# Reordering the weighing of v in a PEER layer: coefficient work, gathers and the loads of v

## The reference, cut to what matters

```
u = peer_u[ix]
a = gelu(einsum('td,thkd->thk', hx, u))
vsel = peer_v[ix]
out = einsum('thk,thkd->td', gx * a, vsel)
```

## Time and profile before

| | |
|---|---|
| median of 3 runs | 3344.83 us (3337.7 to 3346.16) |
| profiled execution | 3339.36 us, its span 3337.5 us |
| TensorE matmuls busy | 2777.6 us, 83% of the span |
| weight loads busy | 1940.9 us, 58% |
| DVE, ScalarE, Pool busy | 1414.0, 847.5, 982.1 us |
| weighing of v, first to last matmul | 1231 to 1777 us |

### The profile page before, as it was taken

The page is one execution under the profiler, slowest core; times in us unless marked ns, Lnnn a source line. Parts: engine busy times, 40 slices in busy tenths (PEclk is TensorE's granted clock), DMA queues, the critical chain, the costliest instruction groups (busy, mean ns, idle before and its releaser), DMA issues. The chain is left out here.

```text
span 3337.5 us, 34889 instructions
## 1 busy us (share of the span) xinstructions
PE 2777.6 (83%) x12909; PEld 1940.9 (58%) x12909; DVE 1414.0 (42%) x2354; ACT 847.5 (25%) x1423; POOL 982.1 (29%) x480
## 2 busy tenths in 40 slices
PE   5985697999999969999995967985788887887886
PEld 3853587998999957777774845664322232222222
DVE  3346527995777755667655254433000000100001
ACT  1224212334666623333333203221100000000001
POOL 0030003667777758887781020000000000000000
PEclk7977798999999989999997975566999999999999
DMA  5343113546999989999993120012899999999996
GB/s 218 103 154 112 69 62 113 170 164 230 335 333 356 350 313 342 341 341 332 334 344 128 57 70 13 1 54 108 349 421 421 422 421 421 421 421 421 421 421 281
DMA packets 267733, 866.91 MB, mean 260 GB/s; under 512 B 30911, under 2 KB 118591, under 8 KB 214968
## 3 DMA queue, kind: packets, MB, share of 16 engines
q1 hardware_dynamic: 211008, 700.59, 55.5%
q0 software_dynamic: 38016, 138.43, 11.0%
q10 hardware_dynamic: 18584, 26.23, 2.1%
HBM read 809.56 MB, written 55.61 MB: 259 GB/s over the span
## 5 line engine op out<-in xcount | busy, mean ns | idle before, releaser
L675 PE MATMUL dots_dot_ps<-one_acts,dots_u_split 128*128 128x384 f32 x3072 | 554.8, 338 | 21.8 <-POOL dots_u_split L87 21.4
L802 PE MATMUL val_banks<-val_v,val_coef_split 128*128 128x512 f32 x2304 | 532.9, 392 | 43.3 <-DVE val_coef_split L87 43.0
L675 PEld LDWEIGHTS dots_dot_ps<-one_acts,dots_u_split 128*128 128x128 f32 x3072 | 532.6, 189 | 29.7 <-issue 22.1
L802 PEld LDWEIGHTS val_banks<-val_v,val_coef_split 128*128 128x128 f32 x2304 | 430.9, 188 | 145.2 <-issue 56.7
L87 POOL TENSOR_TENSOR dots_u_split<-dots_u_raw,dots_u_split 128x1024 fp32r<-128x1024 f32 x128 | 334.4, 2613 | 412.7 <-ACT dots_u_split L82 411.6
L87 POOL TENSOR_TENSOR val_v<-val_v_raw,val_v 128x2048 fp32r<-128x2048 f32 x64 | 297.0, 4641 | 86.9 <-ACT val_v L82 86.9
L1293 PE MATMUL moe_up_ps<-all_raw_first,all_xs_t 128*64 128x512 f32 x1152 | 262.6, 597 | 56.4 <-DMA all_raw_first<-in_w_up 31.8
L1360 DVE TENSOR_TENSOR all_x<-moe_y_ps,all_x 128x512 f32<-128x512 f32 x64 | 44.2, 691 | 565.3 <-PE moe_y_ps L1266 565.3
L1293 PE MATMUL moe_up_ps<-moe_raw_more,all_xs_t 128*64 128x512 f32 x896 | 206.3, 601 | 52.1 <-DMA moe_raw_more<-in_w_up 43.9
L766 DVE SCALAR_TENSOR_TENSOR val_banks<-val_v_rows,one_slot_coef,val_banks 128x1024 f32<-128x1024 f32 x128 | 164.3, 1283 | 189.9 <-DMA val_v_rows<-in_peer_v,one_expert 189.7
L1293 PEld LDWEIGHTS moe_up_ps<-all_raw_first,all_xs_t 128*64 128x64 f32 x1152 | 91.2, 136 | 225.4 <-issue 225.4
(11 more groups left out here) (326 smaller groups left out, 3405.2 us busy)
## 6 DMA issues: line engine op xcount, KB each, us to landing
all_raw_first<-in_w_gate SPq DMA_DIRECT2D x80, 1024.0 KB, 24.1
moe_raw_more<-in_w_down SPq DMA_DIRECT2D x80, 1024.0 KB, 23.8
dots_u_raw<-in_u_tiles SPq DMA_DIRECT2D x128, 512.0 KB, 4.3
val_v_raw<-in_peer_v SPq DMA_DIRECT2D x64, 1024.0 KB, 5.0
all_raw_first<-in_w_up SPq DMA_DIRECT2D x64, 1024.0 KB, 24.1
moe_raw_more<-in_w_up SPq DMA_DIRECT2D x64, 1024.0 KB, 24.9
moe_raw_more<-in_w_gate SPq DMA_DIRECT2D x48, 1024.0 KB, 23.7
all_raw_first<-in_w_down SPq DMA_DIRECT2D x48, 1024.0 KB, 24.8
```

The lines of the kernel that those rows point to most:

```text
L675: last = self.nc.tensor.matmul(self.banks[:, j, 0:DENSE], self.split[:, j, u_part, k], self.h_t[:, h_part, k, T - DENSE:T], start=(k == 0 ...
L802: last = nc.tensor.matmul(banks[:, 2 * (t + 1) + half, :], coef_split[:, b, c_part, a, t * P:(t + 1) * P], v[:, b, v_part, a, half * BANK: ...
```

## The change

In `peer_value_phase`:

- DVE's order becomes: wait for Pool's subtraction t-1, products t, low part t, then the sums of slots 2t-2 and 2t-1; the sums of the last two slots follow the loop.
- Pool gathers slots 2t and 2t+1 behind subtraction t, two slots later than before.
- ScalarE's program is rows 0, and then for each turn coefficients t and rows t+1.
- `coef_split` has three buffers. Dots have semaphores of their own, and the gates come for two turns in one DMA, which stands ahead of the dots in every second turn.
- The buffers lie in `shared` (class `ValueRows`), and the phase is called inside the scope that holds it. SP loads the v rows of turns 0 and 1 at the end of `peer_first_phase`, behind the last tile of u and ahead of the last stores of gates.
- The loops are written out for SP, ScalarE and TensorE too.

In `peer_first_phase` the 128 slots are dealt out over 67 tiles instead of 72.

```diff
--- before.py
+++ after.py
@@ -686,76 +686,72 @@
                       self.gelu[:, j]).then_inc(self.stored[j], 16)
 
 
-def peer_value_phase(nc, A, dots_dram, weight_dram, x, gate, expert, slot_coef, gathered):
+def peer_value_phase(nc, A, dots_dram, weight_dram, x, gate, expert, slot_coef, gathered, values):
 
 
     DT = DENSE // P
     with Scope(nc, "val") as s:
-        v_raw = s.sb("v_raw", [P, 2, 2, D])
+        v_raw, dot, weight, coef, part = values.raw, values.dot, values.weight, values.coef, values.part
         v = s.sb("v", [P, 2, 2, 2, D], F32R)
-        dot = s.sb("dot", [P, 2, 2, DENSE])
-        weight = s.sb("weight", [P, 2, SPANS, 2, SPAN])
-        coef = s.sb("coef", [P, 2, 2, DENSE])
-        coef_split = s.sb("coef_split", [P, 2, 2, 2, DENSE], F32R)
-        part = s.sb("part", [P, 2, BANK])
+        coef_split = s.sb("coef_split", [P, 3, 2, 2, DENSE], F32R)
         sparse = SparseTokens(nc, s, A["peer_v"], expert, "v", gathered)
         banks = s.ps("banks", [P, 8, BANK])
         sparse_sum = banks[:, 0:2, :].rearrange("p a n -> p (a n)")
-        v_loaded = [s.sem(f"v_loaded{i}") for i in range(2)]
-        c_loaded = [s.sem(f"c_loaded{i}") for i in range(2)]
+        v_loaded = values.loaded
+        dot_loaded = [s.sem(f"dot_loaded{i}") for i in range(2)]
+        weight_loaded = [s.sem(f"weight_loaded{i}") for i in range(2)]
         v_hi, v_lo, coef_ready, coef_hi, coef_lo, summed, dve_step, zeroed = (s.sem(x_) for x_ in (
             "v_hi", "v_lo", "coef_ready", "coef_hi", "coef_lo", "summed", "dve_step", "zeroed"))
         n_turns = ETILES // 2
 
-        def turns(eng, body):
-            with eng.Fori(0, n_turns // 2) as i:
-                for b in range(2):
-                    body(i * 2 + b, b, i)
-
         with nc.Block() as block:
             @block.sync
             def _(sp):
-                def load(turn, b, i):
-                    sp.wait_ge(v_lo, turn + 1)
-                    sp.dma_start(v_raw[:, b], A["peer_v"][bass.ds(turn * (2 * P), 2 * P), :].rearrange(
-                        "(a e) d -> e a d", e=P)).then_inc(v_loaded[b], 16)
-                    sp.wait_ge(coef_ready, turn * 2 + 2)
-                    sp.dma_start(dot[:, b], dots_dram[bass.ds(turn * 2, 2)].rearrange(
-                        "a e t -> e a t")).then_inc(c_loaded[b], 16)
-                    sp.dma_start(weight[:, b].rearrange("p s a t -> p s (a t)"),
-                                 weight_dram[:, :, bass.ds(turn * 2, 2), :].rearrange(
-                                     "s b a t -> b s (a t)")).then_inc(c_loaded[b], 16)
-
-                turns(sp, load)
+                for turn in range(n_turns):
+                    b = turn % 2
+                    if turn >= 2:
+                        sp.wait_ge(v_lo, turn - 1)
+                        values.load_rows(sp, turn, b, turn // 2)
+                        sp.wait_ge(coef_ready, 2 * (turn - 1))
+                    if turn % 2 == 0:
+                        pair = turn // 2
+                        sp.dma_start(weight[:, pair % 2].rearrange("p s a t -> p s (a t)"),
+                                     weight_dram[:, :, 2 * turn:2 * turn + 4, :].rearrange(
+                                         "s b a t -> b s (a t)")).then_inc(weight_loaded[pair % 2], 16)
+                    sp.dma_start(dot[:, b], dots_dram[2 * turn:2 * turn + 2].rearrange(
+                        "a e t -> e a t")).then_inc(dot_loaded[b], 16)
 
             @block.scalar
             def _(act):
-                def split(turn, b, i):
-                    act.wait_ge(v_loaded[b], i * 16 + 16)
-                    act.wait_ge(summed, turn + 1)
-                    split_hi(nc.scalar, v[:, b, 0], v_raw[:, b]).then_inc(v_hi, 1)
-                    act.wait_ge(coef_ready, turn * 2 + 6)
-                    split_hi(nc.scalar, coef_split[:, b, 0], coef[:, b]).then_inc(coef_hi, 1)
-
-                turns(act, split)
+                def rows_high(turn):
+                    act.wait_ge(v_loaded[turn % 2], 16 * (turn // 2 + 1))
+                    if turn >= 2:
+                        act.wait_ge(summed, turn - 1)
+                    split_hi(nc.scalar, v[:, turn % 2, 0], v_raw[:, turn % 2]).then_inc(v_hi, 1)
+
+                rows_high(0)
+                for turn in range(n_turns):
+                    act.wait_ge(coef_ready, 2 * turn + 2)
+                    if turn >= 3:
+                        act.wait_ge(summed, turn - 2)
+                    split_hi(nc.scalar, coef_split[:, turn % 3, 0], coef[:, turn % 2]).then_inc(coef_hi, 1)
+                    if turn + 1 < n_turns:
+                        rows_high(turn + 1)
 
             @block.gpsimd
             def _(pool):
-                pool.sem_inc(v_lo, 2)
                 for c in range(sparse.NR):
                     sparse.gather(pool, c)
                 for turn in range(n_turns):
                     b = turn % 2
                     pool.wait_ge(v_hi, turn + 1)
                     split_lo(nc.gpsimd, v[:, b, 1], v_raw[:, b], v[:, b, 0]).then_inc(v_lo, 1)
-                    for c in range(2 * turn + sparse.NR - 2, 2 * turn + sparse.NR):
+                    for c in range(2 * turn + sparse.NR - 4, 2 * turn + sparse.NR - 2):
                         if sparse.NR <= c < P:
                             sparse.gather(pool, c)
 
             @block.vector
             def _(dve):
-                dve.sem_inc(coef_ready, 4)
-                dve.sem_inc(coef_lo, 2)
                 nc.vector.memset(sparse_sum, 0.0).then_inc(zeroed, 1)
                 dve.wait_ge(zeroed, 1)
 
@@ -767,53 +763,56 @@
                         out=sparse_sum, in0=sparse.rows[:, c % sparse.NR, :], scalar=slot_coef[:, c:c + 1],
                         in1=sparse_sum, op0=ALU.mult, op1=ALU.add).then_inc(sparse.used, 1)
 
-                for turn in range(n_turns):
-                    b = turn % 2
-                    dve.wait_ge(c_loaded[b], 32 * (turn // 2 + 1))
-                    dve.wait_ge(coef_lo, turn + 1)
+                def coefficients(turn):
+                    b, pair = turn % 2, turn // 2
+                    dve.wait_ge(dot_loaded[b], 16 * (turn // 2 + 1))
+                    dve.wait_ge(weight_loaded[pair % 2], 16 * (pair // 2 + 1))
+                    if turn >= 2:
+                        dve.wait_ge(coef_lo, turn - 1)
                     for a in range(2):
                         nc.vector.tensor_tensor(
                             coef[:, b, a].rearrange("p (s t) -> p s t", s=SPANS),
                             dot[:, b, a].rearrange("p (s t) -> p s t", s=SPANS),
-                            weight[:, b, :, a, :], ALU.mult).then_inc(coef_ready, 1)
-                    add_slot(2 * turn)
+                            weight[:, pair % 2, :, 2 * (turn % 2) + a, :], ALU.mult).then_inc(coef_ready, 1)
+
+                for turn in range(n_turns):
+                    if turn >= 1:
+                        dve.wait_ge(v_lo, turn)
+                    coefficients(turn)
                     dve.wait_ge(coef_hi, turn + 1)
-                    split_lo(nc.vector, coef_split[:, b, 1], coef[:, b], coef_split[:, b, 0]).then_inc(coef_lo, 1)
-                    add_slot(2 * turn + 1)
+                    split_lo(nc.vector, coef_split[:, turn % 3, 1], coef[:, turn % 2],
+                             coef_split[:, turn % 3, 0]).then_inc(coef_lo, 1)
+                    if turn >= 1:
+                        add_slot(2 * turn - 2)
+                        add_slot(2 * turn - 1)
+                add_slot(P - 2)
+                add_slot(P - 1)
                 step = Steps(dve, dve_step)
                 dve.wait_ge(sparse.used, P)
                 for o in range(8):
                     t, half = o // 2, o % 2
                     cols = slice(half * BANK, (half + 1) * BANK)
                     if o == 2:
-                        dve.wait_ge(summed, 2 + n_turns)
+                        dve.wait_ge(summed, n_turns)
                     step(nc.vector.tensor_tensor(part[:, o % 2, :], banks[:, o, :], gate[:, cols], ALU.mult))
                     nc.vector.tensor_tensor(x[:, t, cols], part[:, o % 2, :], x[:, t, cols], ALU.add)
 
             @block.tensor
             def _(pe):
-                def multiply(turn, b, first=False, final=False):
-                    pe.wait_ge(v_lo, turn + 3)
-                    pe.wait_ge(coef_lo, turn + 3)
+                for turn in range(n_turns):
+                    pe.wait_ge(v_lo, turn + 1)
+                    pe.wait_ge(coef_lo, turn + 1)
                     for a in range(2):
                         for t in range(DT):
                             for c_part, v_part in ((0, 0), (0, 1), (1, 0)):
                                 for half in range(2):
                                     last = nc.tensor.matmul(
-                                        banks[:, 2 * (t + 1) + half, :], coef_split[:, b, c_part, a, t * P:(t + 1) * P],
```

(55 more changed lines are left out.)

## The result

The changed kernel takes 3363.77 us in the median of 7 runs (3360.57 to 3369.34); the kernel before takes 3343.88 on the same chip (3332.25 to 3354.24). The ratio is 1.0067, 95% interval 1.0047 to 1.0086: slower, by about 20 us. The profiled execution took 3360.57 us.

A forecast was written before the change was run, and what follows sets the result against it. The stage was taken as TensorE's, limited by gathers landing late for sums ahead of the coefficients. 28.8 - 3.5 - 3 + 1.2 = +23.5 us gave 3363 or 3368, stated as 3365; own range 3345 to 3384, 8-in-10 range 3312 to 3384.

The forecast's parts named there:

- Reorder: Weighing of v, DVE's new order: turns of 8.95 us, 565.9 us from first to last instead of 537.0, +28.8 us.
- Mode (b): Weighing turns: Pool's subtraction gets in first and the products wait it out; two turns take 17.93 us, 8.97 each.
- the slow start: First turns of the weighing: an allowance of 2 us added to 63 turns of 8.95.
- mode (a): Weighing turns: products get in first; low part, sums, products, subtraction follow one another, 8.8 us a turn, falling into (b).
- Start: Start of the weighing: v rows already in SBUF, TensorE starts 15 us after the stage before instead of 18.5, -3.5 us.
- End of the stage before: Before the weighing: u gathers done earlier, two v loads in their place, 1.25 MB less to move, -3 us (-6 to +3).
- Tail: End of the weighing: last gathers behind the last subtraction, all sixteen DVE output operations after them, +1.2 us (0 to +4).
- Part 5: Gates in pairs, third coefficient buffer, written-out loops: priced 0, +10 if cover for the dots fails on even turns.
- second rival: Weighing at the same rate as now, 8.5 us a turn on average, other parts leaving -5: 3334 to 3340, chance 0.14.
- So the low part t always meets Pool's subtraction t: Weighing turns: the low part, begun after rows t are cast, is always held and ends 0.82 us after Pool.
- The trace has this turn once: Kernel before: one turn cited like (b), TensorE starting 3.06 us after Pool ends, against 2.84 reckoned.
- the 4.2 us of work in the gap: After Pool's subtraction DVE owes low part 0.82, two sums 2.40, products 1.03; the gap has 3.5 us.

The follow-up runs named there:

- e2: Changed kernel with the products taking the dots' operand from PSUM, so only one input is in SBUF (coefficients not the reference's): 3314.9 us.
- e5: Changed kernel without DVE's wait for Pool's subtraction t-1 in front of the products: 3367.9 us.
- e7: Changed kernel with the gates loaded turn by turn instead of in pairs: 3364.6 us.
- e6: Changed kernel with the old order of DVE's work and Pool's gathers, without DVE's new wait: 3355.2 us, ratio to the kernel before 1.0053.
- e1: Changed kernel with the low part reading one input from PSUM, plus DVE waits around it (result not the reference's): 3364.5 us.
- e12: Changed kernel with one added wait, Pool's subtraction t waiting for products t: 3371.1 us.
- e11: e3 with one more wait, Pool's subtraction t waiting for products t+1: 3312.8 us, ratio to the kernel before 0.9920.
- e3: Changed kernel with products a turn ahead, sums 2t-4 and 2t-3 after them, dots and gates loaded earlier: 3369.5 us, ratio to the kernel before 1.0074.
- e4: Changed kernel with sum 2t-3 moved between products t and low part t: 3342.7 us, ratio to the kernel before 1.0007.

## Why the prediction was right

Forecast 3365 us, measured 3363.77, and by the mechanism named. That the two agree to 1.2 us is luck in part: the working gave +23.5 us, the medians differ by 19.9, and 3365 was a choice between 3363 and 3368. Against the span's difference, 3358.6 - 3337.5 = +21.1 us, the terms are:

- **Reorder, +28.8.** Measured 567.9 - 537.0 = +30.8. Mode (b) was priced at 8.97 a turn, and I took 8.95 for an occasional product slipping in ahead, and 2 us for the slow start. From the second turn on the turns came at 9.00, and the first was 0.9 us longer. Products slipped in ahead only in turns 1 and 2, as mode (a), which fell over into (b) at turn 3, as the forecast has it. e2 shows that the hold of the products is the cause, e5 and e7 that the neighbouring edits are not.
- **Start, -3.5.** Measured 13.6 - 17.7 = -4.1. The second product was held already in turn 0, as priced.
- **End of the stage before, -3.** Measured -5.3. No u gather is left after 1186, as forecast. From there to the barrier the DMA engines move 7.61 MB instead of 9.06; the 1.45 MB are 4.3 us at the forecast's 339 GB/s. About 1 us is not accounted for, and no run has the early loads without the 67 tiles or the reverse.
- **Tail, +1.2.** Measured 0: from the last turn's start to the last x it is 1789.62 to 1806.19, 16.6 us, and 1768.15 to 1784.78 before; the two late sums end while TensorE works.
- **Part 5, 0.** It costs nothing in mode (b) (e7 has the same 9.00), whose chain has nothing of it. But it is not free in general: with the old order the same surroundings cost 0.3 us a turn (e6). That I did not see, and 3334 to 3340, as the second rival has it, would have been wrong for the old order in them.

The sum is 30.8 - 4.1 - 5.3 = +21.4. Terms misjudged by 2 us one way and by 4 the other half cancelled.

Three steps of the argument need correction. "So the low part t always meets Pool's subtraction t" is true of mode (a) only: in mode (b) it follows the subtraction (0.96 us, and e1 finds nothing to free). Mode (a) costs 9.08 a turn in e12, not 8.8, so it would have been no way out; the 4.2 us of work in the gap leave out 0.3 of hand-overs. And "The trace has this turn once" counts too few: the kernel before has held products in 14 of its 64 turns.

## What to carry to other kernels

When two in-order engines exclude each other, ask of each schedule not only whether the work fits the gap but which state it returns to after one late start; a hold that shifts the next turn's work into the wrong gap feeds itself. A semaphore wait that makes the long operation come second costs little (22 us in 400 of Pool's slack in e11) and bars that state, but only where the exclusive work is short enough for the gap. And a change that rids an engine of one wait should be priced by the phase in which its other instructions then fall.

## What the runs showed of the hardware

- A product that the record starts ahead of the subtraction can still be the one that waits. In e3 the two begin at 1500.60, 0.91 us ahead, need 1.02, and are held to 0.43 us after Pool's end: the first takes 0.55, the second starts at 1501.07, 0.44 ahead, and takes 5.47. The Trainium skill, "SBUF — State Buffer", says that whichever starts first gets the pair; by the recorded starts that does not hold here. It does hold in e4, where the second product starts 0.05 us ahead and takes 0.55, while the subtraction grows from 4.6 to 4.98:

```profile
1426.76 1.03 DVE L773 TENSOR_TENSOR pe_shared<-pe_shared 128x384 f32<-128x384 f32 x2 [0.44 <-DMA pe_shared<-expert_dots]
1427.29 4.98 POOL L87 TENSOR_TENSOR val_v<-pe_shared,val_v 128x2048 fp32r<-128x2048 f32 x1 [1.36 <-ACT val_v L82]
```

- The traces tell the two cases apart by what Pool did before. In all 58 cases of all runs in which a product recorded ahead was held, the subtraction followed a gather issue within 0.03 us. In the 129 cases in which a product or low part was recorded ahead, would have run into the subtraction and was not held, Pool had stood idle for 0.38 us or more. Why, and how far the recorded start lies from the taking of the pair, no run shows.
- A held product ends 0.41 to 0.43 us after the subtraction, a held low part 0.81 to 0.83. Where the first of two products is held, the second ends 0.88 after.
- Pool's gather issue takes 0.93 to 0.95 us beside a sparse sum. In e3 it takes 1.40 (1509.39) with the low part and the products beside it. Which of these lengthens it was not tested.
